# A two-layer trunk on one core: the second layer's modulation vectors taken from TensorE matmuls to VectorE column sums

## The reference

```python
for l in range(2):
    sh1, sc1, g1, sh2, sc2, g2 = split(silu(c) @ mod_w[l] + mod_b[l], 6)           # mod_w[l] is 1024 x 6144
    csh1, csc1, cg1, csh2, csc2, cg2 = split(silu(c_ctx) @ mod_w[l] + mod_b[l], 6)
    h  = modulate(rms_norm(x, norm1_g[l]), sh1, sc1)
    hc = modulate(rms_norm(cx, norm1_g[l]), csh1, csc1)
    o, oc = even_mixer(h, hc, ...) if l == 0 else odd_mixer(h, hc, ...)            # attention + convolution, or attention + scan
    x = x + g1 * o
    x = x + g2 * swiglu(modulate(rms_norm(x, norm2_g[l]), sh2, sc2), ffn_w_in[l], ffn_w_out[l])
    # layer 0 does the same for cx with csh2, csc2, cg2
return x
```

## Time and profile before

| | us |
|---|---|
| runs | 1188.58, 1189.69, 1187.94 |
| the profiled execution's own time | 1187.6 |
| its span | 1185.8 |
| PE busy | 1157.7 (98%) |
| DVE busy | 693.6 (58%) |
| ACT busy | 485.3 (41%) |
| layer 0's feed-forward on PE | from 314 to 683 |

### The profile page before, as it was taken

How to read it: one execution, slowest core, us unless ns; L and a number is a source line. 1 busy time by engine, 2 the same in 40 slices (tenths; PEclk the granted TensorE clock), 3 DMA queues, 4 the chain that set the end, 5 groups by cost and what they waited for, 6 DMA issues and landing times.

```text
span 1185.8 us, 17766 instructions
## 1 busy us (share of the span) xinstructions
PE 1157.7 (98%) x7266; PEld 934.1 (79%) x7266; DVE 693.6 (58%) x1159; ACT 485.3 (41%) x744; POOL 13.9 (1%) x20
## 2 busy tenths in 40 slices
PE   8999999999999999999999999999999999999998
PEld 5777766777588888888887767899565898998997
DVE  5699978853643334423323368887789645554455
ACT  3423336552433232222212242367268636443442
POOL 3000000000000000000000000000000000000000
PEclk9999999999999999999999999999999999999999
DMA  9845473125543222332123664344140157655551
GB/s 346 316 152 177 159 251 122 36 82 203 184 139 104 88 76 84 125 123 84 67 80 116 206 198 142 95 119 143 36 143 2 47 178 239 213 177 179 193 167 65
DMA packets 118893, 167.73 MB, mean 141 GB/s; under 512 B 4797, under 2 KB 102695, under 8 KB 114599
## 3 DMA queue, kind: packets, MB, share of 16 engines
q1 hardware_dynamic: 118390, 166.23, 42.1%
q10 hardware_dynamic: 433, 0.51, 0.2%
HBM read 164.37 MB, written 1.05 MB: 139 GB/s over the span
## 4 chain that ended last, share of the span: by engine, by line
PE 85%; DVE 10%; ACT 2%; DMA 2%; issue 1%; SPq 0%; DVEq 0%; ACTq 0%; POOL 0%
PE acc L2153 20%; PE acc L2154 20%; PE acc L2155 20%; PE pmod L2073 2%; PE acc L2232 2%; PE acc L2233 1%; PE acc L2234 1%; PE p L2518 1%; PE p L2519 1%; PE p L2517 1%; DMA first_mod<-in_mod_w 1%; PE p L2006 1%; DVE Y L1429 1%; DVE sm L1511 1%; PE p L2395 1%
## 5 line engine op out<-in xcount | busy, mean ns | idle before, releaser
L646 DVE TENSOR_TENSOR w_lo<-raw,w_hi 128x1024 fp32r<-128x1024 f32 x222 | 249.0, 1163 | 234.8 <-ACT w_hi L636 234.5
L636 ACT ACTIVATE w_hi<-raw 128x1024 fp32r<-128x1024 f32 (+1 forms) x224 | 212.8, 998 | 408.7 <-PE acc L2155 358.2
L2153 PE MATMUL acc<-Hhi,w_hi 128*128 128x512 f32 (+1 forms) x960 | 326.3, 340 | 1.6 <-DVE w_lo L646 1.6
L2155 PE MATMUL acc<-Hhi,w_lo 128*128 128x512 f32 (+1 forms) x960 | 324.3, 338 | 0.0
L2154 PE MATMUL acc<-Hlo,w_hi 128*128 128x512 f32 (+1 forms) x960 | 324.2, 338 | 0.0
L2153 PEld LDWEIGHTS acc<-Hhi,w_hi 128*128 128x128 f32 x960 | 182.1, 190 | 25.7 <-issue 3.9
L2155 PEld LDWEIGHTS acc<-Hhi,w_lo 128*128 128x128 f32 x960 | 182.1, 190 | 19.6
L2154 PEld LDWEIGHTS acc<-Hlo,w_hi 128*128 128x128 f32 x960 | 182.2, 190 | 19.2
L2153 PE MATMUL acc<-hid_hi,w_hi 128*128 128x512 f32 x248 | 97.9, 395 | 0.1
L2154 PE MATMUL acc<-hid_lo,w_hi 128*128 128x512 f32 x248 | 96.6, 390 | 0.0
L2155 PE MATMUL acc<-hid_hi,w_lo 128*128 128x512 f32 x248 | 96.6, 389 | 0.0
(11 more groups left out here) (392 smaller groups left out, 1602.8 us busy)
## 6 DMA issues: line engine op xcount, KB each, us to landing
raw<-in_mod_w SPq DMA_DIRECT2D x44, 1024.0 KB, 5.3
raw<-in_ffn_w_in SPq DMA_DIRECT2D x44, 1024.0 KB, 5.1
raw<-in_od_w_in SPq DMA_DIRECT2D x15, 1024.0 KB, 5.4
raw<-in_ffn_w_out SPq DMA_DIRECT2D x12, 768.0 KB, 4.5
raw<-in_ev_w_in SPq DMA_DIRECT2D x8, 1024.0 KB, 7.5
raw<-in_od_w_out SPq DMA_DIRECT2D x8, 1024.0 KB, 5.9
raw<-in_ffn_w_out SPq DMA_DIRECT2D x8, 1024.0 KB, 5.0
raw<-in_ev_w_out SPq DMA_DIRECT2D x8, 768.0 KB, 6.3
```

The lines of the kernel that those rows point to most:

```text
L636: nc.scalar.activation(w_hi[:, w % 2, c0:c1], raw[:, r % RAW_SLOTS, c0:c1], ACT.Copy)\
L646: nc.vector.tensor_tensor(w_lo[:, w % 2, c0:c1], raw[:, r % RAW_SLOTS, c0:c1], w_hi[:, w % 2, c0:c1].bitcast(F32), ALU.subtract).then_inc( ...
L2153: mm(outs[m], hi[:, j, cols], xh, start=(first and j == 0), stop=False)
L2155: ins = mm(outs[m], lo[:, j, cols], xh, start=False, stop=(last and j == kts - 1))
```

## The change

Layer 0's modulation stays with `mod_unit`. Of its group 2, only four units stay in attention A (in the form with 256 columns, `MOD_STEPS` and `MOD_TURN` of 4), and the other four, which make the second gate, go into norm 1, ahead of `ffn(0)` (`GATE_UNITS`: three in its first place, one inside the first products). Layer 1's modulation leaves `mod_unit` and the ring. It is done in four sweeps. A sweep is 32 loads of a piece of 128 rows by 512 columns (256 KB) into one of two buffers, `piece`, and 32 DVE operations, `columns`, each of which scales the piece's rows by the partition's own element of `cvec` and adds it to `col_acc` (128x2048). Sweeps 0 and 1 read the same columns of `mod_w` for the two vectors, 2 and 3 the other groups, so the pieces are 32 MB in all, where the units' loads were 24 MB. After each sweep `sweep_sum` on PE sums the partitions by four matmuls with a one-hot matrix of 32 columns. `PIECES_AFTER[b]` says how many piece loads SP issues after weight block b of `ffn(0)`, `PAIR_PIECES` and `OUT_PIECES` how many `columns` DVE does at which place. A piece load waits until the piece two before it has been used (`piece_used`).

```diff
+        SWAPPED = (3 * 64, 2 * 64)
+        def piece_of(n):
+            i = n % 32
+            return n // 32, 2 * (i // 16) + i % 2, i % 16 // 2, i % 2
...
+            def load_pieces(count):
+                for n in range(pieces[0], pieces[0] + count):
+                    sweep, q, k, e = piece_of(n)
+                    if n < 2:
+                        sp.wait_ge(s("conv_dve"), BT * B_CONV)
+                    else:
+                        sp.wait_ge(s("piece_used"), n - 1)
+                    col = SWEEPS[sweep][0] + 512 * q
+                    sp.dma_start(piece[:, e, :], a["mod_w"][1, k * P:(k + 1) * P, col:col + 512])\
+                        .then_inc(s(f"side_loaded{e}"), 16)
+                pieces[0] += count
+            def load_ffn_0():
+                b = 0
+                for r in range(FF[0][0], FF_END[0]):
+                    load(r)
+                    if stream[r][0] == "w":
+                        load_pieces(PIECES_AFTER.get(b, 0))
+                        b += 1
...
+            def columns(count):
+                for n in range(taken[0], taken[0] + count):
+                    sweep, q, k, e = piece_of(n)
+                    v = SWEEPS[sweep][1]
+                    if n % 32 == 0 and sweep:
+                        dve.wait_ge(mod_used, 3 * KD + sweep)
+                    dve.wait_ge(s(f"side_loaded{e}"), SWAPPED[e] + 16 * (n // 2 + 1))
+                    o, c = col_acc[:, 512 * q:512 * q + 512], cvec[:, k, v:v + 1]
+                    if k == 0:
+                        ins = V_.tensor_scalar(o, piece[:, e, :], c, None, ALU.mult)
+                    else:
+                        dve.wait_ge(s("piece_used"), n - 1)
+                        ins = V_.scalar_tensor_tensor(out=o, in0=piece[:, e, :], scalar=c, in1=o, op0=ALU.mult, op1=ALU.add)
+                    ins.then_inc(s("piece_used"), 1)
...
                         split(w + q + 1, it)
+                        columns(pieces[0])
                         dve.wait_ge(block_done, at(w + q + 1, it, 4))
...
                         V_.tensor_tensor(lo, f_h[:, :, 0:t], hi.bitcast(F32), ALU.subtract).then_inc(s("hid_lo_done"), 1)
+                        columns(pieces[1])
...
                     if half == 0:
-                        mod_final(3)
-                        with dve.Fori(0, 2) as it:
-                            for q in range(4):
-                                split(w + q + 2, it)
-                                if q % 2:
-                                    dve.wait_ge(block_done, at(w + q + 1, it, 4))
-                                    update(l, G2, q // 2, 2 * (q // 2), t, it)
+                        for q in range(8):
+                            split(w + q + 2)
+                            columns(OUT_PIECES[0][q])
+                            if q % 2:
+                                dve.wait_ge(block_done, w + q + 1)
+                                update(l, G2, (q // 2) % 2, 2 * (q // 2), t)
+                        mod_copy(4)
                     else:
+                        mod_copy(5)
                         for q in range(8):
                             if q:
                                 split(w + q + 1)
+                            if q == 1:
+                                mod_final(5)
+                            columns(OUT_PIECES[1][q])
...
+            def sweep_sum(n):
+                v = SWEEPS[n][1]
+                pe.wait_ge(s("piece_used"), 32 * (n + 1))
+                pe.wait_ge(s("mod_ready"), (4, 4, 5, 6)[n])
+                for g in range(4):
+                    ins = mm(pmod[32 * g:32 * g + 32, :], cst("headA", 15 - v, 47 - v), col_acc[:, g * 512:(g + 1) * 512],
+                             start=(n != 1), stop=(n != 0))
+                ins.then_inc(mod_used, 1)
...
+                        if l == 0 and q == 0:
+                            sweep_sum(2 * half)
...
                         with pe.Fori(0, 2) as it:
                             for q in range(4):
                                 ffn_out(w, q, it, 2, q // 2)
+                        sweep_sum(1)
                     else:
                         for q in range(8):
                             ffn_out(w, q, None, 0, q // 2)
-                            if 2 <= q < 2 + MOD_EARLY:
-                                mod_unit(4 * KD + q - 2)
+                            if q == 0:
+                                mod_T(5)
...
-MOD_STEPS = {u: u for u in range(8)}
-MOD_TURN = 8
-MOD_EARLY = 3
-MOD_WAIT = ((3, 4, 5), (6, 7))
-MOD_LAST = ((0, 1, 2), (3,))
+MOD_STEPS = {u: u for u in range(4)}
+MOD_TURN = 4
+GATE_UNITS = ((4, 5, 6), (7,))
+SWEEPS = ((0, 0), (0, 1), (MOD_COLS, 0), (2 * MOD_COLS, 0))
+PAIR_PIECES = (((4, 4),) * 4 + ((0, 0), (0, 8)), ((4, 4),) * 4 + ((0, 8),))
+OUT_PIECES = ((3,) * 8, (4,) * 6 + (0, 0))
+PIECES_AFTER = {3: 8, 5: 8, 7: 8, 9: 8, 13: 8, **{b: 3 for b in range(14, 22)}, 23: 8, 25: 8, 27: 8, 29: 8, 31: 12,
+                **{b: 4 for b in range(32, 37)}}
```

More of the change, by code:

```diff
@@ L291, in build_trunk @@
         probTC = view("probTC", [2, 2, T], r_h + 12288)
+        col_acc = view("col_acc", [2048], r_misc + 16384)
+        piece = view("piece", [2, 512], r_misc + 24576)
         f_gate = view("f_gate", [2, T], r_misc)
@@ L369, in add_ffn @@
                         stream.append(("w", ffn_in[l], 0, KD, side * FFN + P * t0 + BC * p_, BC))
-                        if half == 0 and p_ == 0:
-                            stream.extend(("mod", 1, 0, k) if l == 0 else ("mod", 1, 2, k + 4)
-                                          for k in (MOD_WAIT, MOD_LAST)[l][side])
+                        if l == 0 and half == 0 and p_ == 0:
+                            stream.extend(("mod", 0, 2, k) for k in GATE_UNITS[side])
                 if l == 1:
@@ L380, in add_ffn @@
                         stream.append(("w", ffn_out[l], t0 + part * nt // 2, nt // 2, BC * m, BC))
-                        if l == 0 and half and 2 <= 2 * m + part < 2 + MOD_EARLY:
-                            stream.append(("mod", 1, 1, 2 * m + part - 2))
         add_ffn(0)
@@ L618, in _ @@
                 for c in range(LT):
-                    sp.wait_ge(*((s("out_first"), c + 1) if half == 0 else (s("out_ready"), c + 1)))
+                    sp.wait_ge(s("out_ready"), LT * half + c + 1)
                     cols = slice(512 * half, 512 * half + 512)
@@ L1226, in _ @@
             square0(6)
-            GROUPS = [(l, j) for l in range(DEPTH) for j in range(3)]
+            GROUPS = {1: (0, 1), 4: (1, 0), 5: (1, 1), 6: (1, 2)}
             def mod_first(f0):
@@ L1647, in ffn, with up @@
                     R = FFN_READS[l][2 * half]
-                    def up(w, q, it, pair, per, hi, lo):
+                    def up(w, q, it, pair, per, hi, lo, pieces=(0, 0)):
                         split(w + q + 1, it)
+                        columns(pieces[0])
                         dve.wait_ge(block_done, at(w + q + 1, it, 4))
@@ L1773, in _ @@
             norm(2, T, C_IN + 1)
-            mod_copy(4)
+            mod_copy(6)
             w = C_IN
@@ L1991, in _ @@
             norm(3, LAT, FF[1][1] + 1)
-            mod_copy(6)
             ffn(1, LAT)
@@ L2090, in mod_T @@
                 pe.wait_ge(s("modc_ready"), n + 3)
-                for b in range(4 if n < 5 else 2):
+                for b in range(2 if n in (2, 3) else 4):
                     ins = T_(pmod[:, b * P:(b + 1) * P], modc[:, b * P:(b + 1) * P])
@@ L2426, in square_sums @@
                 if q == 7:
-                    fill = [KD * (n + 2) + k + 4 * (n == 3) for k in (MOD_LAST if n == 3 else MOD_WAIT)[0]]
-                    for m in fill[:1]:
-                        mod_unit(m)
+                    fill = GATE_UNITS[0] if n == 1 else ()
+                    for k in fill[:1]:
+                        mod_unit(2 * KD + k)
+                    if n == 2:
+                        sweep_sum(3)
                     spread_roots(n, t)
-                    for m in fill[1:]:
-                        mod_unit(m)
+                    for k in fill[1:]:
+                        mod_unit(2 * KD + k)
             def second_weights(n, w):
@@ L2557, in ffn @@
                     w += 4 * n_in
+                    if l == 0 and half:
+                        mod_T(4)
                     for q in range((nt - 2 * alone) % 4):
                         up_or_gate(w, q, None, nt // 2 - 1, 0)
+                        if l == 0 and q == 0:
+                            sweep_sum(2 * half)
                     w += (nt - 2 * alone) % 4
@@ L2839, in _ @@
                     sum_y(b - 1)
-            for k in (0, 1):
-                mod_unit(KD * 5 + k)
             sum_y(3)
```

114 lines of the change are left out of this document (54 added, 60 removed).

## The result

The changed kernel takes 1255.9 us (median of 4 runs, 1252.3 to 1259.8); the kernel before takes 1188.3 (now 4 runs, 1187.6 to 1189.7). The ratio is 1.0575, with a 95% interval of 1.0561 to 1.0589. I had forecast 1221 and a range up to 1240: slower as I said, but by 68 us and not by 33. The profiled execution took 1252.3 us, with a span of 1250.5 and a mean granted clock of 0.974 (before: 0.999).

What follows compares the result with a forecast made beforehand. PE, busy 98% of the span, was taken as the bound. 1187.6 less 15.6 us removed, plus 3.3 added PE work, waits of 2.1, 3.8, 16.2, 7.4 and 14.0, and 1.7 of clock: 1220.5, stated as 1221; range 1196 to 1240.

Steps and rivals of the forecast that it cites:

- block 14's wait: Half 0's feed-forward: eight pieces after block 13's load delay block 14's load, so PE waits 2.1 us.
- blocks 15 to 19: Half 0's output part: a turn takes 8.9 us against PE's 8.2, a wait at each block, 3.8 us in all.
- the sum at half 0's end: sweep_sum(1), ahead of half 1's first block, waits for piece 63 behind split(21): 16.2 us, 7.3 with all loads early.
- the turn of group 4: After block 30, PE's mod_T(5) waits for mod_copy(5), behind hid_lo and eight columns on DVE: 7.4 us.
- half 1's output blocks: Blocks 32 to 37: a turn takes 9.0 us against PE's 6.8, a wait at each block, 14.0 us in all.
- clock, over the kernel before's: After PE's one idle time of 16 us, the granted clock is lower for a while: 1.7 us lost.
- gain in attention C (with its clock): Copy, turn and gains leave DVE in attention C, where PE waited 0.98 us for DVE: 1.0 us gained.
- The order on SP: Feed-forward output parts: the next weight load is issued behind a piece waiting for a column after the split; three-block lead gone.
- The landings: DMA loads in the feed-forward: 2.4 us for a 256 KB piece, bounds 2.0 and 4.6; weight loads 4.5 and 4.3.
- The rival for the clock: Half 1's output part: clock falls to half, 4.6 us more for each of six blocks, 1249 us; chance 0.04.
- In norm 2 the two at 686.53 cost nothing: Norm 2: removing these two units gains nothing, as PE waits another 1.06 us behind them for Hlo.
- DVE's work: 128 column operations on DVE at 0.66 us, 84 us in all, hidden by work alone in 14.7 us idle a pair.

Runs made afterwards that it cites:

- the large pieces: Changed kernel with later sum, later piece loads and early mod_copy(5), plus pieces of 128x1024 (512 KB), half as many: 1190.9 us, 1.0017 of before.
- the dummy units in the feed-forward's waits: Changed kernel plus 33 units of matmuls with unused results on PE where it waits in the feed-forward: 1246.8 us, 1.0503 of before.
- the new schedule with the units: Changed kernel with 512 KB pieces, sums, turns and copies a block or more later, and seven dummy units in norm 2, attention C, norm 3: 1176.4 us.
- those at the old places: Changed kernel plus seven units of matmuls with unused results on PE, where norm 2, attention C and norm 3 had real ones: 1247.0 us, 1.0498 of before.
- the sum later: Changed kernel with sweep_sum(1) moved behind half 1's second block and mod_copy(4) behind block 22's split: 1246.3 us, 1.0498 of before.
- thin columns: Changed kernel with DVE column operations after a sweep's first two of each column block cut to 16 of 512 columns: 1231.7 us, 1.0375 of before.
- thin loads: Changed kernel with piece loads after the first two cut to 128 of 512 columns (64 KB), all DVE columns kept: 1225.2 us, 1.0314 of before.

## Why the prediction was right in kind and wrong in size

| Term of the sum | forecast | in the trace |
|---|---|---|
| PE's gain ahead of the feed-forward | 7.2 | 7.0 (8.2, less 1.2 at the start) |
| block 14's wait | 2.1 | 5.5 |
| blocks 15 to 19 | 3.8 | 4.8 |
| the sum at half 0's end | 16.2 | 17.7 |
| the turn of group 4 | 7.4 | 10.0 |
| half 1's output blocks | 14.0 | 10.4 |
| waits for the gate's ACT, and at `sweep_sum(2)` | 0 | 4.7 |
| clock, over the kernel before's | 1.7 | 19.3 |
| gain in attention C (with its clock) | 1.0 | -2.0 |

The last two rows overlap: the loss in attention C holds 3.4 us that also stand in the row of the clock, so without its clock attention C gained 1.4. The waits come to 43.5 us in my sum and 53.0 in the trace. With the overlap taken out, the rows explain 27 of the 32 us by which my sum is short of the profiled execution. The other 5 us I haven't placed.

- **The order on SP** was right. The chain above is the one that the prediction spells out, and moving the pieces behind two more loads took 44.6 us.
- **The sum at the end of half 0** and **the turn of group 4** were right in place and within 1.5 and 2.6 us in size. That the sum's wait is a cost of its own was half wrong: taken away alone, it gave 10 us, because the update stood in the same late chain. The turn's gave 2, no more than the spread of the runs.
- **The landings** are mis-sized. I had a piece at 2.4 and the weight loads at 4.5 and 4.3 plus 0.4 us; under this traffic they took 3.0, 5.7 and 5.5. Of the 53.0 us of waits, 4.7 stand at two kinds of place to which I had given nothing. The bound of 4.6 that I kept for a piece came from a load with rows of 128 bytes, and the median of 3.0 stayed well under it. The 2.6 us of the Trainium skill (DMA: Bandwidth & Descriptors, the anatomy of one DMA) was nearer than my 2.4, and still short of the trace; for 512 KB its fit gives an estimate of 3.2 where the large pieces took 4.0 and more. The waits of block 32 and those behind it came out smaller (10.4 against 14.0), though the turns were longer than forecast. I had a wait at each block from 32 to 37; the trace has them at 32, 33, 35 and 37, and at 34 and 36 only 0.5 and 0.6 us for ACT. PE at blocks 33, 34, 35 and 37:

```profile
697.17 0.71 PE L2213 MATMUL acc<-hid_hi,w_hi 128*128 128x512 f32 x1 [3.14 <-DVE w_lo L672]
...
706.36 0.95 PE L2169 MATMUL p<-n_sq,const 128*32 128x128 f32 x16 [0.47 <-ACT n_sq L769]
...
716.49 0.50 PE L2213 MATMUL acc<-hid_hi,w_hi 128*128 128x512 f32 x1 [2.17 <-DVE w_lo L672]
...
737.04 0.50 PE L2213 MATMUL acc<-hid_hi,w_hi 128*128 128x512 f32 x1 [3.29 <-DVE w_lo L672]
```

From 697 to 706 and from 716 to 725 PE lost 1.5 and 1.7 us to the lower clock. It came that much later to blocks 34 and 36, whose splits were by then under way. So some of the row of the clock stands in place of waits; the rows say where PE's time went and not what each cause alone would cost.

- **The clock** is the step that failed. "a fifth of 5 us and of some more gives 1.7 us lost" priced one fall, after the longest wait. The trace has nine behind waits, of 5.5, 17.7, 10.0, 3.1, 2.2, 3.3, 2.9, 2.3 and 1.7 us, and each costs 1.5 to 3.4 us. It is 17.6 us more than my sum has, the largest difference in the table. That most of it is real time is shown by the dummy units in the feed-forward's waits: 11 us less of clock loss, 9 us less of time. The rival for the clock stood at 0.04 and was wrong in form: the clock didn't stay low through half 1's output part, it fell and rose at each long wait. The Trainium skill, TensorE: Matmul & The Clock Gate, in the section on HAM oscillation, has this: a wait in each turn of a loop, and the clock low at each turn's start. I had noted it and gave it no place in the sum; the trace agrees with it (clock down to 0.50 and 0.56 behind 3.1 and 3.3 us in the output blocks).
- **"In norm 2 the two at 686.53 cost nothing"** The earlier trace rows was true and misleading. A unit beside a wait costs nothing, and taking it away gains nothing by time; but the wait that it covered grew from 1.06 to 2.9 us, and the clock fell behind it. In attention C two pairs of units covered such waits. My sum has no term for these four units, and gives no reason for that. It counts a gain of 1.0 for the copy, the turn and the gains, by a wait of 0.98 that I read as theirs; it was for `probC` and stands in the changed kernel too. In place of the gain came a loss of 2.0 (the same products of PE start 63.7 us later than before ahead of attention C and 65.7 behind it). The seven dummy units give 5.3 us back.
- **DVE's work** was right: the second of two columns in a row adds 0.66 us (two take 1.41), and the 128 columns are busy for 88.0 us in all (84 forecast). It is hidden wherever the schedule asks for it early.

The nearest thing to a measured sum of parts is the new schedule with the units: 11.5 us under the kernel before, near the 12.3 us that the prediction gave for the change without any wait. The comparison is fair, as the seven units stand where my sum had counted 0.3 us at most for taking units away. That the two agree within 1 us is partly luck, since the terms of norms and attention C were wrong one by one.

## What to carry to other kernels

Work moved to an idle engine is free only if nothing in order waits for it just after it was asked for: look at each queue that it passes, put its loads behind those that bound the kernel, its results a block ahead of their reader, and make its transfers large enough that landing doesn't show. A wait that is taken away alone comes back at the next thing that the same late chain owes, so follow the chain and not the gap. And before taking small work off TensorE, look at what it covers: on this kernel every wait of 2.9 us and more had some 1.5 to 2.9 us of lost clock behind it, and so had many of 1.7 to 2.7, so filler that computes nothing can be worth its place.

## What the runs showed of the hardware that was not expected

- The fall of the clock isn't the same in each run for waits between 1.7 and 2.7 us. In the changed kernel no fall follows waits of 1.83 (at 422) and 2.27 (at 647), and one follows 2.17 (at 716) and 1.73 with one of 1.44 just ahead (at 1056). With the dummy units in the feed-forward no fall follows 2.57 and 2.51; with those at the old places one follows 1.80. With the sum later, none follows 2.69. In three of the fourteen traces a fall stands in norm 1, behind waits of 1.27 and 0.61. All waits of 2.9 us and over had one.
- With that goes the spread of the times. The changed kernel's four runs lie 7.4 us apart, the kernel before's 2.1, and those of the last kernel, whose clock never falls behind a wait, 0.9. The changed kernel's runs of 1252.3 and 1255.1 us had a mean granted clock of 0.974, those of 1256.7 and 1259.8 one of 0.966 and 0.967. But the kernels with thin columns and thin loads lie only 2.0 and 2.5 us apart, with eight and seven falls in their traces. So falls alone don't make the spread. That it comes from falls that some executions have and others not is likely, and wasn't tested.
- Weight loads beside 256 KB pieces landed 1.2 us later (5.7 and 5.5 in place of 4.5 and 4.3), although the mean rate in the feed-forward rose only from 114 to some 160 GB/s, less than half of the 350 that the first windows of the run reach. With 64 KB pieces the 640 KB loads landed in 4.4. The traffic is not all of it: in the run with large pieces, where the same bytes move in another order, the 768 KB loads landed in 4.5 and the 640 KB ones in 6.5. Why is open.
